# VectorE takes all eight dots of the last group of block 1 in a two-layer convolution, attention and expert kernel

## The reference

```
xb: (128 tokens, D) of one block; eb, gb: (128, 8, 16) experts and gates
u = u_tab[eb]
h = einsum("thkd,td->thk", u, xb)
coef = gb * gelu(h)
out = einsum("thkd,thk->td", v_tab[eb], coef)
```

## Time and profile before

| | |
|---|---|
| median of 3 runs | 3294.75 us (3293.91 to 3295.1) |
| profiled execution, its own time | 3293.62 us |
| its span in the profile | 3291.9 us |
| TensorE busy | 2867.3 us (87%) |
| VectorE busy | 2474.6 us (75%) |
| GpSimd busy | 1549.9 us (47%) |
| ScalarE busy | 824.0 us (25%) |
| mean granted clock of TensorE | 0.943 of full |
| DMA, mean over the span | 337 GB/s |

### The profile page before, as it was taken

One profiled execution on the slowest core, in us unless ns is written; L12 is line 12 of the kernel. 1 busy time (PEld: TensorE's weight loads), 2 busy tenths in 40 slices (PEclk: granted clock), 3 DMA queues, 4 the chain that ended last, 5 costly groups with the idle time before them and its releaser, 6 DMA issues.

```text
span 3291.9 us, 44647 instructions
## 1 busy us (share of the span) xinstructions
PE 2867.3 (87%) x15083; PEld 2203.4 (67%) x15083; DVE 2474.6 (75%) x3647; ACT 824.0 (25%) x1268; POOL 1549.9 (47%) x1317
## 2 busy tenths in 40 slices
PE   9999987677777899999899999977768777999997
PEld 8887886666777644444697977966667776444443
DVE  6996698999999766666543545898999998766666
ACT  1015422123433500000233544322124334200000
POOL 0000567777677644444200002677766676544443
PEclk9999998888898999999999999988889889999999
DMA  8434499999999899999755434799999999999998
GB/s 259 154 128 155 157 362 422 422 421 415 415 419 419 310 406 405 409 409 407 270 207 179 129 141 153 261 410 422 421 421 418 417 417 353 376 409 407 410 409 342
DMA packets 293996, 1108.20 MB, mean 337 GB/s; under 512 B 22068, under 2 KB 120948, under 8 KB 220788
## 3 DMA queue, kind: packets, MB, share of 16 engines
q0 software_dynamic: 147456, 805.37, 60.4%
q1 hardware_dynamic: 146420, 301.26, 25.3%
HBM read 1104.45 MB, written 2.10 MB: 336 GB/s over the span
## 4 chain that ended last, share of the span: by engine, by line
DMA 39%; PE 27%; DVE 16%; issue 9%; POOL 6%; ACT 2%; POOLq 0%; DVEq 0%; ACTq 0%
DMA ring<-in_peer_u,index_now 18%; DMA work<-in_peer_v,index_add 15%; PE ps L857 7%; PE ps L754 5%; DVE ring L1862 5%; PE ps L797 5%; DMA more_add<-in_peer_v,index_add 5%; POOL ring L597 4%; DVE ps L1934 3%; PE ps L808 2%; PE ps L936 1%; PE ps L1040 1%; DMA ring<-in_peer_w_q 1%; DMA work<-in_peer_v,index_v 1%; PE ps L1080 1%
## 5 line engine op out<-in xcount | busy, mean ns | idle before, releaser
L597 POOL DMA_INDIRECT ring<-in_peer_u,index_now x480 | 786.7, 1639 | 351.9 <-issue 140.2
L1862 DVE SCALAR_TENSOR_TENSOR ring<-ring,x_tok 128x2048 f32<-128x2048 f32 x372 | 844.0, 2290 | 101.7 <-DMA ring<-in_peer_u,index_now 91.4
L1093 PE MATMUL ps<-all_v,mix 128*128 128x512 f32 x1984 | 851.8, 592 | 0.0
L1093 PEld LDWEIGHTS ps<-all_v,mix 128*128 128x128 f32 x1984 | 377.0, 190 | 474.5 <-issue 474.5
L1046 PE MATMUL ps<-x_dot,work 128*128 128x128 f32 x3968 | 521.0, 294 | 113.0 <-DVE ps L1869 69.9
L1934 DVE SCALAR_TENSOR_TENSOR ps<-work,coef,ps 128x1024 f32<-128x1024 f32 x330 | 424.1, 1289 | 245.7 <-DMA work<-in_peer_v,index_add 213.9
L1046 PEld LDWEIGHTS ps<-x_dot,work 128*128 128x128 f32 x3968 | 498.7, 208 | 142.4 <-issue 69.6
L581 POOL TENSOR_TENSOR w_lo<-ring,w_hi 128x512 fp32r<-128x512 f32 x104 | 134.1, 1325 | 828.8 <-ACT w_hi L1226 804.0
L1396 ACT ACTIVATE work<-ps 128x1024 f32<-128x1024 f32 x248 | 243.9, 1022 | 611.5 <-PE ps L1040 582.5
L706 POOL DMA_INDIRECT work<-in_peer_v,index_add x272 | 257.4, 946 | 289.0 <-DVE ps L1934 215.3
L1624 DVE TENSOR_TENSOR w_lo<-ring,w_hi 128x2048 fp32r<-128x2048 f32 x85 | 194.8, 2292 | 245.5 <-ACT w_hi L1226 245.5
(11 more groups left out here) (234 smaller groups left out, 3766.1 us busy)
## 6 DMA issues: line engine op xcount, KB each, us to landing
all_v<-in_peer_v SPq DMA_DIRECT2D x248, 512.0 KB
ring<-in_peer_w_q SPq DMA_DIRECT2D x16, 2048.0 KB, 9.3
ring<-in_attn_w_kv SPq DMA_DIRECT2D x16, 2048.0 KB, 8.7
ring<-in_conv_w_in SPq DMA_DIRECT2D x14, 2048.0 KB, 9.2
ring<-in_conv_w_out SPq DMA_DIRECT2D x8, 2048.0 KB, 7.5
ring<-in_attn_w_q SPq DMA_DIRECT2D x8, 2048.0 KB, 8.6
ring<-in_attn_w_o SPq DMA_DIRECT2D x8, 2048.0 KB, 7.4
ring<-in_peer_u,index_now POOLq DMA_INDIRECT x480
```

The costliest lines, as they stand in the source:

```text
L597: pool.indirect_dma_start(tile, None, u_tab, bass.IndirectOffsetOnAxis(ap=index_now[:, half, s:s + 1], axis=0)).then_inc(landed_in, 16)
L1093: mm = pe.matmul(ps[:, dense_bank(tb, q), :], mix[tb][:, row, :], tile[:, q * 512 - HALF:(q + 1) * 512 - HALF], start=False, stop=True, sk ...
L1862: dve.scalar_tensor_tensor(out=tile, in0=tile, scalar=1.0, in1=x_tok[:, tb, :], op0=ALU.mult, op1=ALU.mult, accum_out=coef[:, tb, slot]).t ...
```

## The change

In the last group of block 1 the ring's tiles 0 and 4 are no longer turned. VectorE makes plain dots of them (`closing_dots`), counted by the new `last_used`; TensorE and ScalarE leave their loops a group earlier and do only the last `mix_pair` behind them. GpSimd's wait for the rooms of half rows 2 to 5 now names the group before the last. Since a layer now has one turned group less than ring groups, the counts of `h_steps`, `h_taken`, `u_turned` and `u_taken` are worked out with a `turn_group` of their own.

```diff
+        def turn_group(layer, tb):
+            return layer * (RING_GROUPS - 1) + tb * GROUPS - 1
...
                 for n in range(G_RING):
                     if n == 2:
-                        pool.wait_ge(h_steps, 2 + 2 * NT * RING_GROUPS * (layer + 1))
+                        pool.wait_ge(h_steps, 2 + 2 * NT * (RING_GROUPS - 1) * (layer + 1))
                     gather_add(n)
...
-                with pe.Fori(2 * DOUBLE, GROUPS) as i:
+                with pe.Fori(2 * DOUBLE, GROUPS - 1) as i:
                     mix_pair(i, 1, 0)
                     turned_dots(1, i)
+                mix_pair(GROUPS - 1, 1, 0)
...
-                    act.wait_ge(h_taken, NT * (1 + done))
+                    act.wait_ge(h_taken, NT * (1 + turn_group(layer, tb) + GROUPS - tb))
+                    if tb:
+                        act.wait_ge(last_used, NT * (layer + 1))
...
-                with act.Fori(2 * DOUBLE, GROUPS) as i:
+                with act.Fori(2 * DOUBLE, GROUPS - 1) as i:
                     weigh_pair(i, 1, 0)
                     take_turned(1, i)
-                act.wait_ge(u_taken, 2 + (layer + 1) * 2 * NT * RING_GROUPS)
+                weigh_pair(GROUPS - 1, 1, 0)
+                act.wait_ge(u_taken, 2 + (layer + 1) * 2 * NT * (RING_GROUPS - 1))
...
+                def closing_dots():
+
+                    group = GROUPS - 1
+                    for s in range(U_RING):
+                        slot = group * U_RING + s
+                        if s in TURNED:
+                            e = TURNED.index(s)
+                            take_dot(1, e, 2 * ((turn_group(layer, 1) + group - 1) * NT + e) + 4, slice(slot - U_RING, slot - U_RING + 1))
+                        dot(1, u_tile(s), u_row[s], group * 16 + row_at(layer, 1), slice(slot, slot + 1), last_used if s in TURNED else u_used)
...
-                        dots(1, p, p + 1)
+                        if p == GROUPS - 1:
+                            closing_dots()
+                        else:
+                            dots(1, p, p + 1)
                     else:
                         half_group(1, 2 + p // 2, p % 2)
                 dve.wait_ge(mix_ready, (layer + 1) * BATCHES)
-                for e in range(NT):
-                    last_dot(1, e)
                 weights(1)
```

More of the change, by code:

```diff
@@ L285, in build @@
         index_copied, pool_tick = sem("index_copied"), sem("pool_tick")
-        u_used = sem("u_used")
+        u_used, last_used = sem("u_used"), sem("last_used")
         dot_x_turned, dot_x_taken = sem("dot_x_turned"), sem("dot_x_taken")
@@ L617, in gather_group @@
                         copy_numbers(half, tb, bass.ds(i * (2 * U_RING) + slot, U_RING), i * 2 + copies)
+                    turned = turn_group(layer, tb) + group
                     for s in range(U_RING):
-                        gather_tile(half, s, n * (2 * NT) if i is None else i * (4 * NT) + n * (2 * NT),
+                        gather_tile(half, s, turned * (2 * NT) if i is None else i * (4 * NT) + turned * (2 * NT),
                                     n * ND if i is None else i * (2 * ND) + n * ND)
@@ L1033, in turned_dots @@
                         s = TURNED[e]
-                        n = ring_group(layer, tb) * NT + e
+                        n = turn_group(layer, tb) * NT + e
                         pe.wait_ge(u_row[s], i * 16 + row_at(layer, tb))
@@ L1857, in peer, with dot @@
                     x_low(1 + 2 * layer, tb)
-                def dot(tb, tile, landed_in, landed_at, slot):
+                def dot(tb, tile, landed_in, landed_at, slot, used=u_used):
                     dve.wait_ge(landed_in, landed_at)
                     dve.scalar_tensor_tensor(out=tile, in0=tile, scalar=1.0, in1=x_tok[:, tb, :],
-                                             op0=ALU.mult, op1=ALU.mult, accum_out=coef[:, tb, slot]).then_inc(u_used, 1)
+                                             op0=ALU.mult, op1=ALU.mult, accum_out=coef[:, tb, slot]).then_inc(used, 1)
                 def take_dot(tb, e, steps, slot):
@@ L1882, in dots @@
                 def dots(tb, first, last):
-                    base = ring_group(layer, tb)
+                    turned = turn_group(layer, tb)
                     with dve.Fori(first, last) as i:
@@ L1888, in dots @@
                                 e = TURNED.index(s)
-                                take_dot(tb, e, i * (2 * NT) + (2 * ((base - 1) * NT + e) + 4), bass.ds(i * U_RING + s - U_RING, 1))
+                                take_dot(tb, e, i * (2 * NT) + (2 * ((turned - 1) * NT + e) + 4), bass.ds(i * U_RING + s - U_RING, 1))
                             else:
@@ L1899, in half_group @@
                             slot = (group - 1) * U_RING + s
-                            take_dot(tb, e, 2 * ((base + group - 1) * NT + e) + 4, slice(slot, slot + 1))
+                            take_dot(tb, e, 2 * ((turned + group - 1) * NT + e) + 4, slice(slot, slot + 1))
                         else:
@@ L1907, in last_dot @@
                     s = TURNED[e]
-                    take_dot(tb, e, 2 * ((ring_group(layer, tb) + GROUPS - 1) * NT + e) + 4,
+                    take_dot(tb, e, 2 * ((turn_group(layer, tb) + GROUPS - 1) * NT + e) + 4,
                              slice(SLOTS - U_RING + s, SLOTS - U_RING + s + 1))
+                def closing_dots():
[6 more added lines that the diff above has]
+                        dot(1, u_tile(s), u_row[s], group * 16 + row_at(layer, 1), slice(slot, slot + 1), last_used if s in TURNED else u_used)
                 def first_dots(first, last):
```

## The result

The changed kernel takes 3299.44 us (median of 20 runs, 3295.26 to 3304.01) where the kernel before, run beside it, takes 3294.5 (20 runs, 3289.92 to 3297.01). The ratio is 1.0014, with a 95% interval of 1.0009 to 1.0020: 4.9 us slower, a difference that so many runs do show, but under the 0.2% that the prediction took as the least that counts. The forecast was 3299.7.

What follows compares the result with a forecast made beforehand. The prediction took the chain from dots through coefficients to the rounds, then TensorE's dense pass, as the bound. Adding 0.28 + 0.27 + 2 x 2.2 = 4.95 us to the median of 3294.75 gave 3299.7 us, range 3294.8 to 3303.0.

Steps and rivals of the forecast that it cites:

- The early half rows: Before the rounds: four half rows of v asked for earlier bring 0; bounds 0 and 5 us gained per layer.
- the early rows do help: Rival, in the rounds or early dense pass: less waiting for landings gains 2 x 5.0 us; chance 0.09.
- a dense pass bound by TensorE: Argument against early rows helping: behind the rounds TensorE is busy 430.00 of 430 us at full clock.
- The eight dots: Last group of block 1: VectorE's eight dots end later, +0.28 us in layer 0 and +0.27 in layer 1.
- The rival of late tiles: Asks for v delay slots 5 to 7 of u by up to 5.0 us; 3309.7 us in all; chance 0.08.
- The clock: TensorE idles some 11 us before the coefficients, then runs the next burst at half clock: +2.2 us per layer.
- A count of work alone: Sum without the clock's term, in which fewer matmuls on TensorE can only help: 0.55 us in all.
- That the loss goes through: Whatever moves the start of the rounds moves the layer's end by as much, once for each of two layers.
- the clock's loss doesn't reach the path: Rival: idle stretches in the rounds absorb the clock's loss, leaving only 0.55 us, 3295.3 us; chance 0.13.
- sign of being wrong: The prediction is wrong if the stretch from the first round to the layer's end changes its length.
- The sum: Both layers together: 0.28 + 0.27 + 2 x 2.2 = 4.95 us slower, a median of 3299.7 us; chance 0.70.

Runs made afterwards that it cites:

- e2_late_asks: Changed kernel, but GpSimd asks for half rows 2 to 5 of v only after VectorE's last dot; 3299.3 us, 1.0016 of the kernel before.
- e0_after_again: The changed kernel measured once more with no edit; 3299.14 us, 1.0016 of the kernel before.
- e1c_warm: Changed kernel plus 11 spare matmuls on TensorE between first residual and turning of the last coefficients; 3294.08 us, 0.9999 of the kernel before.
- e3_order: Changed kernel with the second residual placed ahead of the turning of the coefficients, no spare matmuls; 3295.46 us, 0.9999 of the kernel before.
- e1_warm: Changed kernel plus 26 spare matmuls on TensorE between first residual and turning of the last coefficients; 3316.04 us, 1.0069 of the kernel before.

## Why the prediction was right

**The early half rows.** Taken at 0, measured at 0.2 us in the medians of e2_late_asks and e0_after_again and 0.2 to 0.4 us for each layer in D3. The rival "the early rows do help" is refuted for this kernel at its size of 5 us for each layer. The DMA rate in 1085 to 1142 fell from 320 to 298 GB/s as the half rows moved out of it, and the rounds ran no faster from the third on. The hole in the DMA's work was moved and became longer. One argument against this rival was too strong, though: "a dense pass bound by TensorE". TensorE is busy all through it and then still waits 3.63 us for gathered half rows, so that landings do count there; it is e2_late_asks that rules the rival out.

**The eight dots.** Predicted +0.28 and +0.27 us, measured 18.19 - 18.01 = 0.18 in each layer. The dots start 0.21 behind the taken dot, not 0.32, as the lower bound had allowed for. That VectorE would end the group by itself, past the landings, was right.

**The rival of late tiles.** Refuted: with six asks behind them the last dots still ran at 2.21 without a wait for a landing.

**The clock.** Predicted 2.2 us for each layer in a range of 1.5 to 2.9, measured 6.23 - 3.58 = 2.65 and 5.95 - 3.58 = 2.37. The full clock came back some 5 us after the burst began (by 1085 for a burst from 1079.62, and between 2771 and 2772 for one from 2766.35), inside the 3.1 to 5.8 read from the earlier trace rows. That this is the cause is shown from both sides: the same instructions at full clock behind spare work (e1c_warm, 3.57 us, no loss of time that the interval shows), and less work in the cold burst (e3_order). The idle time was taken at 11 us and was 12.8. The rule of the Trainium skill that was weighed ("TensorE: Matmul & The Clock Gate", section "Why this matters for your kernels") held here: behind 12.8 idle us the next burst ran at half clock. A count of work alone would have said 0.55 us.

**That the loss goes through.** The rounds kept their length from the third on, and 4.7 us at the third rounds stand against 4.9 in the medians. The rival "the clock's loss doesn't reach the path" is refuted. The prediction's sign of being wrong, another length from the first round to the layer's end, did not come in layer 0 (514.57 us before, 514.63 after); the stretch scatters by more than that.

**The sum** had 4.95 us and the medians differ by 4.94. That they agree so well is luck. In sum the dots were 0.2 us too high and the clock 0.6 too low, and the first two rounds gave back 0.6 us that the prediction, which had the start of the rounds move the end by as much, did not count. The interval of the ratio alone leaves 3.0 to 6.6 us.

One misreading did not reach the sum: I took L830's and L1080's records for single matmuls of 0.43 us. The prediction used the duration of the whole groups only.

## What to carry to other kernels

Work that is taken off an engine may have been its cover: before counting TensorE's saved matmuls as free, ask what it does in their place and what it must do right behind, since the first burst on the path can pay for the idle time at half clock. Data that arrives sooner is worth something only if someone was waiting for it; ask for the wait in the rows before filling a hole in the DMA's work. And idle time that a change makes is a resource: with independent work moved into it, spare matmuls to keep the clock up and the early asks, a loss of 0.14% became a gain of 0.13%.

## What the runs showed of the hardware

GpSimd's indirect DMA instruction takes 0.94 to 1.02 us beside VectorE's masks and adds or beside nothing, and 1.9 to 2.2 beside VectorE's dots over 2048 elements; with the dots back to back the asks fall into their step, 2.21 us apart (1064.10, 1066.31). The dots themselves stay at 2.28 us. A matmul of the program with 512 columns in fp32 is recorded as two instructions (56 records for 28 in e1_warm) and takes 0.86 us at full clock and 1.71 at half (1079.86 to 1083.28 for two). A wait of 3.40 us behind 11.43 us of matmuls left TensorE's clock full (e1c_warm, layer 1), and one of 12.8 us did not.
